# A two-block transformer layer in fp32 split products: weight splits placed first in each step, the second output projection ended tile by tile, the first expert's pieces in another order

## The chip, the cores and the metric

The kernel runs on one core of a Trainium2 chip. The metric is the device time of one execution in microseconds; the version before takes 806.64 us (median of three runs, 806.54 to 807.74). All times below are microseconds; those of the profile count from the start of the profiled execution's span.

## The reference

Two blocks in a row on 256 tokens of width 1024, in fp32. The first block (attention and retention, a convolutional feed-forward part) isn't touched by the change. The second ends like this:

```python
merged = gate_a * (o_a @ w_proj_a[l]) + gate_b * (o_b @ w_proj_b[l])
x = x + merged @ w_out[l]
x = x + hier_moe(rmsnorm_2(x, norm2_g[l]), w_router_group[l], b_router_group[l],
                 w_router_expert[l], b_router_expert[l], w_exp_gate[l], w_exp_up[l], w_exp_down[l])
return rmsnorm_2(x, final_norm_g)
```

`hier_moe` gives each token one of 4 groups by the router's group logits and weights of its two best experts within the group; each of the 16 experts is a gated unit (1024 to 256 twice, and 256 back to 1024).

## The kernel before

**Products.** A product in fp32 precision is three TensorE matmuls on rounded parts: `hi*hi`, `lo*hi`, `hi*lo` (`three`). For each weight quarter (128x1024 numbers) ScalarE writes the rounded `w_hi`, then another engine writes the rest, `w_lo = raw - w_hi`. Up to the end of the output projection GpSimd does the latter (L669); for the experts VectorE does (L3044), with ScalarE's part at L746. The matmuls of a quarter wait for its `lo`.

**Order.** Each engine has its own instruction list, written out by hand; engines meet by semaphores. An engine takes its list strictly in order, so an instruction whose semaphore is late holds all behind it.

**Output projection and router.** The second output projection (`token_quarter`, L1285) has 8 quarters of 12 matmuls for two tiles of 128 tokens (t = 0, 1) and two halves of the width (c = 0, 1; banks 2, 3 and 0, 1). After the seventh quarter TensorE transposes half c = 0 of `x` (`turn_half`, L1388), and after the eighth it runs the router products of k = 0 to 3 (L2025, L2027), transposes c = 1, and runs the router products of k = 4 to 7. VectorE adds the bank to `x` (L2425) and writes `h_lo` (L2242), ScalarE writes `h_hi` (L772). Matmuls whose results nobody reads (`keep_warm`, L1487) stand after the router and after the counting.

**Choice of groups.** From the logits VectorE finds each token's group (L2993 to L3019), TensorE counts the tokens of each group (`count_tokens`, L2042 to L2046), VectorE ranks the groups (L3023 to L3026) and sets `ranks_ready`. ScalarE and VectorE each load the rank's number into a register; ScalarE then splits the first expert's weights (L736, L738) and VectorE follows (L3037, and L3044 for its second quarter). After that VectorE works out each token's place in the sorted order (L3051 to L3060), the `one_hot` matrices (L3062) and the experts' weights (to L3100). Meanwhile ScalarE scales the rows of `x` (L1181), rounds them (L1184), and GpSimd writes their `lo` (L693). TensorE sorts the tokens with the one-hot matrices (`gather`, L2055).

**Experts.** There are 20 units (an expert with a tile of tokens; n = 0 to 19) and 120 steps p. A step is six matmuls of 128x512. Steps (n, 0) to (n, 3) are the up projections of unit n, (n, 4) and (n, 5) the down projections. After (n, 3) ScalarE takes the SiLU (L1208) and VectorE the product (L3122); TensorE transposes it (`turn_act`, L2100), ScalarE copies it (L1214) and VectorE writes its `lo` (L3128), for which (n, 4) waits. Between these pieces both engines split the quarters to come: quarter j at step `SPLIT_AT[j]`. A ring of 8 quarters holds them, so that j waits on ScalarE until quarter j - 8 is used up. Mostly one quarter is due per step. Units 6 and 7 (and 12 and 13) use the same weights one after the other; after these the ring frees late, and steps 53 and 89 have five splits each, 43 to 47 and 73 to 77. The transposes of units 8 and 14 stand at steps 54 and 90.

Of the kernel before, what the change touches and what calls it, by code (L numbers as in the profile page):

```python
# [141 lines left out]
GATHER_STEP = 4  # L142

# [211 lines left out]
def program(nc, weights, smalls, x_in, p_in, vec_in, rows, con_in, slot_in, pos_in, out):  # L355

    ctx = ExitStack()
    with ctx:
# [349 lines left out]
        def _(act_e):  # L708
# [458 lines left out]
            def left_squares(t):  # L1167

                act_e.wait_ge(sem("pair_free1"), 40)
                nc.scalar.activation(tok3[:, t, 0:512], x3[:, t, 0:512], ACT.Square, scale=D ** -0.5,  # L1170
                                     accum_out=stat[:, 8 + t:9 + t]).then_inc(sem("left_squares"), 1)

            for t in range(NT):
                left_squares(t)
            prepare_root()
            norm_hi(4, "norm2", range(4, KD))
# [95 lines left out]
        def _(pe):  # L1272
# [736 lines left out]
            for n, (c, f) in enumerate(WOUT2_ORDER):  # L2009
                if f == 0:  # L2010
                    await_pair(39 + c)
                pe.wait_ge(sem("merged_lo_done"), f + 1)
                token_quarter(4 * B_WOUT2 + n, 39 + c, f, (h_hi, h_lo))
                if n == 6:
                    await_read(39)
                    turn_half(4, 0)

            def router(ks):

                for k in ks:  # L2020
                    pe.wait_ge(sem("h_lo_done"), KD * 4 + k // 2 * 2 + 2)
                    at = slice(KD * 24 + 20 * k, KD * 24 + 20 * (k + 1))
                    for t in range(NT):
# [25 lines left out]
            keep_warm(1, 8, warm)  # L2049
# [123 lines left out]
        def _(dve):  # L2173
# [789 lines left out]
            def right_squares(t):  # L2963

                x = x3[:, t, 512:D]
                dve.wait_ge(sem("pair_free0"), 41 + t)
                link(V.tensor_tensor_reduce(tok3[:, t, 512:D], x, x, 1.0 / D, 0.0, ALU.mult, ALU.add, stat[:, t:t + 1]))
# [3 lines left out]
            add_pair(4 * B_WOUT2 + WOUT2_ORDER.index((1, 3)) + 1, 40, 1)  # L2971
            for t in range(NT):
                right_squares(t)
            dve.wait_ge(sem("left_squares"), NT)
            V.scalar_tensor_tensor(last_sums, stat[:, 8:10], RMS_EPS, stat[:, 0:2], ALU.add, ALU.add).then_inc(sem("last_summed"), 1)
            norm_lo(4, "norm2", range(4, KD))
# [12 lines left out]
            dve.wait_ge(sem("h_lo_done"), 5 * KD)  # L2989
# [56 lines left out]
            slot_low_first(chosen)  # L3046
            slot_low(1, chosen)

# [10 lines left out]
            link(V.tensor_tensor(near_place, place, near_rank, ALU.mult))  # L3059
            link(V.tensor_reduce(routed("slot"), near_place, AX_X, ALU.add))  # L3060
# [85 lines left out]
            for p in range(4, len(STEPS) - 1):  # L3146
                for n in range(len(UNITS)):
# [7 lines left out]
                if p == 5:  # L3155
                    slot_h_second(range(4, KD))
                for j in range(4, len(STREAM)):
                    if p == SPLIT_AT[j]:
                        slot_low(j)
                if p == step_of(0, 4):  # L3160
                    store_slot_weights()

# [60 lines left out]
```

## Time and profile before

| | |
|---|---|
| time, three runs | 806.64 (806.54 to 807.74) |
| the profiled execution's own time | 806.66 |
| its span | 804.7 |
| TensorE busy | 786.0 (98% of the span) |
| VectorE, ScalarE, GpSimd busy | 467.7, 435.8, 449.4 |
| mean granted TensorE clock | 0.993 of full speed |

The span is what the profiler saw between first and last instruction; the 1.96 us around it belong to the time too. TensorE's busy time includes matmuls that stream slowly, so the granted clock has to be read beside it.

### The profile page before, as it was taken

The numbers are of one execution on the slowest core, as the hardware profiler recorded it, in microseconds if no ns is written. First come the engines' busy times: TensorE is split into PE (matmuls) and PEld (weight loads), VectorE is DVE, ScalarE is ACT, GpSimd is POOL, SyncE is SP. The second block draws the span as 40 slices with busy tenths as digits, with TensorE's granted clock in tenths as the row PEclk, the third lists the DMA queues.
The fourth block names the chain that finished last, engine by engine and source line by source line (L and its number), as shares of the span: only waits on it lengthen the run. The fifth ranks groups of instructions, "written<-read, shape, count | busy, mean of one in ns | idle before, by whom it ended". The sixth has DMA issues, their size and how long they took to land.

```text
span 804.7 us, 15723 instructions
## 1 busy us (share of the span) xinstructions
PE 786.0 (98%) x6063; PEld 704.7 (88%) x6063; DVE 467.7 (58%) x947; ACT 435.8 (54%) x680; POOL 449.4 (56%) x351
## 2 busy tenths in 40 slices
PE   8999999999999999999999999999999899999996
PEld 7998889999999998889999999999978688788784
DVE  5853454672412215486498944437736896795874
ACT  5434654745545456785549534234427675673753
POOL 4997486999999998878974524245832000000002
PEclk9999999999999999999999999999998999999998
DMA  8765145455654555445663312233455796696811
GB/s 299 269 210 210 57 154 184 162 205 209 209 207 161 205 202 169 155 154 177 197 202 127 106 55 75 86 107 106 151 202 235 310 384 272 244 391 236 313 72 52
DMA packets 22810, 151.29 MB, mean 188 GB/s; under 512 B 2656, under 2 KB 3168, under 8 KB 5344
## 3 DMA queue, kind: packets, MB, share of 16 engines
q1 hardware_dynamic: 21312, 147.26, 50.2%
q10 hardware_dynamic: 1440, 3.21, 1.4%
q8 instruction: 42, 0.69, 0.3%
q14 instruction: 16, 0.13, 0.1%
HBM read 147.97 MB, written 1.05 MB: 185 GB/s over the span
## 4 chain that ended last, share of the span: by engine, by line
PE 93%; DVE 3%; ACT 1%; issue 1%; DMA 1%; ACTq 0%; DVEq 0%
PE bank L1285 77%; PE bank L1856 3%; DVE w_lo L3044 1%; PE bank L1388 1%; PE bank L1438 1%; PE bank L1452 1%; DMA vec<-vectors_dram 1%; PE bank L2100 1%; PE bank L1487 1%; PE bank L1885 0%; PE bank L1944 0%; PE bank L1866 0%; PE bank L2141 0%; PE bank L1461 0%; PE bank L1462 0%
## 5 line engine op out<-in xcount | busy, mean ns | idle before, releaser
L669 POOL TENSOR_TENSOR w_lo<-raw,w_hi 128x512 fp32r<-128x512 f32 x340 | 439.6, 1332 | 151.3 <-ACT w_hi L721 141.3
L1285 PE MATMUL bank<-h_hi,w_hi 128*128 128x256 f32 x800 | 227.3, 284 | 0.0
L1285 PE MATMUL bank<-h_hi,w_lo 128*128 128x256 f32 x800 | 222.3, 278 | 0.0
L1285 PE MATMUL bank<-h_lo,w_hi 128*128 128x256 f32 x788 | 218.4, 277 | 0.0
L721 ACT ACTIVATE w_hi<-raw 128x1024 fp32r<-128x1024 f32 x170 | 173.6, 1059 | 64.9 <-PE bank L1285 34.6
L1285 PEld LDWEIGHTS bank<-h_hi,w_hi 128*128 128x128 f32 x800 | 150.5, 188 | 4.2 <-issue 1.7
L1285 PEld LDWEIGHTS bank<-h_hi,w_lo 128*128 128x128 f32 x800 | 150.4, 188 | 0.0
L1285 PEld LDWEIGHTS bank<-h_lo,w_hi 128*128 128x128 f32 x788 | 148.1, 188 | 0.3
L1285 PE MATMUL bank<-w_hi,g 128*128 128x512 f32 x360 | 115.7, 391 | 3.4 <-issue 1.8
L700 POOL TENSOR_TENSOR tok<-x_sb,work 128x512 f32<-128x512 f32 x2 | 2.5, 1286 | 184.4 <-DVE x_sb L3166 184.4
L1285 PEld LDWEIGHTS bank<-w_hi,g 128*128 128x128 f32 x360 | 67.6, 188 | 18.2 <-issue 2.3
L1285 PE MATMUL bank<-w_hi,h_hi 128*128 128x512 f32 x184 | 73.4, 399 | 0.7 <-DVE w_lo L3037 0.6
L1285 PE MATMUL bank<-w_hi,h_lo 128*128 128x512 f32 x184 | 72.3, 393 | 0.0
L1285 PE MATMUL bank<-w_lo,h_hi 128*128 128x512 f32 x184 | 72.0, 392 | 0.0
L1285 PE MATMUL bank<-w_lo,g 128*128 128x512 f32 x180 | 70.2, 390 | 0.0
L2446 DVE TENSOR_TENSOR bank<-bank,work 128x512 f32<-128x512 f32 x11 | 7.7, 697 | 70.3 <-PE bank L1285 70.3
L3044 DVE TENSOR_TENSOR w_lo<-work,w_hi 128x1024 fp32r<-128x1024 f32 x39 | 45.7, 1220 | 3.0 <-ACT w_hi L746 2.6
L1285 PEld LDWEIGHTS bank<-w_hi,h_hi 128*128 128x128 f32 x184 | 34.6, 188 | 8.8 <-DVE w_lo L3037 1.0
L1285 PEld LDWEIGHTS bank<-w_hi,h_lo 128*128 128x128 f32 x184 | 34.6, 188 | 7.4
L1285 PEld LDWEIGHTS bank<-w_lo,h_hi 128*128 128x128 f32 x184 | 34.6, 188 | 6.9
L1285 PEld LDWEIGHTS bank<-w_lo,g 128*128 128x128 f32 x180 | 33.8, 188 | 6.6
L3044 DVE TENSOR_TENSOR w_lo<-raw,w_hi 128x1024 fp32r<-128x1024 f32 x32 | 37.7, 1219 | 2.8 <-ACT w_hi L746 2.6
(422 smaller groups left out, 1316.8 us busy)
## 6 DMA issues: line engine op xcount, KB each, us to landing
raw<-weights_dram SPq DMA_DIRECT2D x109, 1024.0 KB, 4.8
work<-weights_dram SPq DMA_DIRECT2D x27, 1024.0 KB, 6.8
x_sb<-x_dram SPq DMA_DIRECT2D x2, 512.0 KB, 4.5
raw<-weights_dram SPq DMA_DIRECT2D x2, 512.0 KB, 7.1
work<-final_norm_dram ACTq DMA_DIRECT2D x2, 512.0 KB, 4.3
work<-work ACTq DMA_DIRECT2D x8, 128.0 KB, 6.6
out_dram<-tok SPq DMA_DIRECT2D x3, 256.0 KB, 2.2
work<-constants_dram SPq DMA_DIRECT2D x1, 640.0 KB, 7.0
```

The lines of the kernel that those rows point to most:

```text
L669: return nc.gpsimd.tensor_tensor(w_lo[:, part], raw[:, part], w_hi[:, part].bitcast(F32), ALU.subtract)
L700: nc.gpsimd.tensor_tensor(tok3[:, 0, of], x3[:, 0, of], norm_row2[:, of], ALU.mult).then_inc(sem("first_gained"), 1)
L721: nc.scalar.activation(w_hi[:, ring(q)], raw[:, ring(q)], ACT.Copy).then_inc(sem("hi_done"), 1)
L1285: ins = mm(dst, a, b, start=start and n == 0, stop=stop and n == 2, skip_group_check=True)
L1388: ins = nc.tensor.transpose(bank[turned_bank(n, k)][:, k % 2 * S + t * P:k % 2 * S + (t + 1) * P], x3[:, t, k * P:(k + 1) * P], ident)
L1438: ins = mm(bank[4 + odd][:, t * P:t * P + (t + 1) * P], q3[own, f, t * P:(t + 1) * P], k3[own, kf(f), 0:(t + 1) * P], start=True, stop=True)
L1452: ins = nc.tensor.transpose(bank[6 + n % 2][:, i * P:(i + 1) * P], p[:, i * P:(i + 1) * P], ident)
L1487: mm(bank[to][:, 0:x.shape[1]], x[:, 0:P], x, start=True, stop=True, skip_group_check=True)
L1856: ins = mm(bank[b][rows, column + m * w:column + (m + 1) * w], lhs[rows, m, :], rhs[rows, m, :], start=True, stop=True)
L2100: ins = nc.tensor.transpose(to[:, k * P:(k + 1) * P], slot_act[:, k * P:(k + 1) * P], ident)
L2446: V.tensor_tensor(u_, u_, root_rows, ALU.mult).then_inc(sem("root_applied"), 1)
L3044: V.tensor_tensor(lo_, of, hi_.bitcast(F32), ALU.subtract).then_inc(sem("slot_lo_done"), 1)
```

## The change

Three things, and some small ones that go with them.

1. From step 10 on (`OPENED`), the splits of a step stand ahead of the other pieces of that step on ScalarE and VectorE. Before, they stood last.
2. The output projection's last two quarters of half c = 1 are done tile by tile: first tile 0 of both quarters, then tile 1, with the transposes of half c = 0 and of tile 0 between. `x`, `h_hi`, `h_lo` and the second half of the router follow tile by tile; ScalarE takes over tile 1's square of that half. The `keep_warm` behind the counting has 11 matmuls, not 8.
3. On VectorE, the arithmetic of the places stands ahead of the first expert's two quarters; in the first steps the product of unit 0 stands ahead of splits 4 and 5 and of the second half of `slot_lo`.

```diff
 # ScalarE, before the experts
+            act_e.wait_ge(sem("pair_free1"), 40)
+            for t in range(NT):
+                part_square(t, 0, stat[:, 8 + t:9 + t])
+            prepare_root()
             norm_hi(4, "norm2", range(4))
...
-            norm_hi(4, "norm2", range(4, KD))
+            act_e.wait_ge(sem("norm_turned"), 19)
+            for k in range(4, KD):
+                tile_hi(0, k, 6, k - 4)
+            act_e.wait_ge(sem("pair_free0"), 42)
+            part_square(1, 1, stat[:, 1:2])
+            for k in range(4, KD):
+                act_e.wait_ge(sem("norm_turned"), 20 + (k - 4) // 2)
+                tile_hi(1, k, (7, 0)[(k - 4) // 2], k % 2)
 # ScalarE, experts (VectorE has the same with slot_low)
             for p in range(4, len(STEPS) - 1):
+                splits = [j for j in range(4, len(STREAM)) if p == SPLIT_AT[j]]
+                if p >= OPENED:
+                    for j in splits:
+                        slot_hi_quarter(j)
                 for n in range(len(UNITS)):
...
-                for j in range(4, len(STREAM)):
-                    if p == SPLIT_AT[j]:
+                if p < OPENED:
+                    for j in splits:
                         slot_hi_quarter(j)
 # TensorE
+            for f in (2, 3):
+                ins = token_half(4 * B_WOUT2 + 4 + f, 40, f, 0)
+            ins.then_inc(sem("tile_ready"), 1)
+            await_read(39)
+            turn_half(4, 0)
+            token_half(4 * B_WOUT2 + 6, 40, 2, 1)
+            turn_tile(0, (6,))
+            token_half(4 * B_WOUT2 + 7, 40, 3, 1)
...
-            router(range(4))
-            await_read(40)
-            turn_half(4, 1)
-            router(range(4, KD)).then_inc(sem("logits_ready"), 1)
+            router(range(4), range(NT), lambda k: k // 2 * 2 + 2)
+            turn_tile(1, (7, 0))
+            router(range(4, KD), (0,), lambda k: 8)
+            router(range(4, KD), (1,), lambda k: 8 + (k - 4) // 2 * 2 + 2).then_inc(sem("logits_ready"), 1)
             keep_warm(1, 6, warm)
...
-            keep_warm(1, 8, warm)
+            keep_warm(1, 11, warm)
...
                     if n == 1:
                         pe.wait_ge(sem("slot_weights_ready"), 1)
-                        pe.wait_ge(sem("slot_h_lo"), KD)
 # VectorE, places and first expert
-            slot_low_first(chosen)
-            slot_low(1, chosen)
-
             dve.wait_ge(sem("counted"), 2)
             counts = bank[2][:, 0:NT * GROUPS].rearrange("p (t n) -> p t n", t=NT)
             V.tensor_tensor(near_place, counts, group_one, ALU.mult)
...
             link(V.tensor_tensor(near_place, place, near_rank, ALU.mult))
+            slot_low_first(chosen)
+            slot_low(1, chosen)
             link(V.tensor_reduce(routed("slot"), near_place, AX_X, ALU.add))
...
-                if p == 5:
-                    slot_h_second(range(4, KD))
-                for j in range(4, len(STREAM)):
-                    if p == SPLIT_AT[j]:
-                        slot_low(j)
                 if p == step_of(0, 4):
                     store_slot_weights()
+                if p == step_of(0, 5):
+                    slot_h_second(range(4, KD))
+                if p < OPENED:
+                    for j in [4] * (p == step_of(0, 3) + 1) + [5] * (p == step_of(0, 4)) + splits:
+                        if j not in (4, 5) or p > 6:
+                            slot_low(j)
```

The first place of which the prediction speaks is VectorE's list behind the ranking of the groups. `TENSOR_LOAD` is the load into the register, the `ISA` rows belong to it and to the address that it gives. Before:

```order
L3026 TENSOR_SCALAR work<-work 128x4
L3029 TENSOR_LOAD work
L3029 ISA x2
L3037 ISA
L3037 TENSOR_TENSOR w_lo<-work,w_hi 128x512
L3037 ISA
L3037 TENSOR_TENSOR w_lo<-work,w_hi 128x512
L3044 ISA
L3044 TENSOR_TENSOR w_lo<-work,w_hi 128x1024
L3051 TENSOR_TENSOR bank<-bank,work 128x8
L3052 TENSOR_TENSOR bank<-work 128x2x4
L3053 TENSOR_REDUCE work<-bank 128x2
```

The same place on VectorE after the change, with line numbers of the changed kernel:

```order
L3075 TENSOR_LOAD work
L3075 ISA x2
L3094 TENSOR_TENSOR bank<-bank,work 128x8
L3095 TENSOR_TENSOR bank<-work 128x2x4
L3096 TENSOR_REDUCE work<-bank 128x2
L3097 TENSOR_REDUCE work<-bank 128x2
L3099 TENSOR_TENSOR bank<-work 128x2x4
L3100 TENSOR_TENSOR bank<-work 128x8
L3101 TENSOR_TENSOR work<-bank,work 128x8
L3102 TENSOR_TENSOR bank<-work,bank 128x8
L3083 ISA
L3083 TENSOR_TENSOR w_lo<-work,w_hi 128x512
```

Eight small operations moved from behind the two quarters to ahead of them. Three of them (`bank<-work`) have both inputs in SBUF; so has `w_lo<-work,w_hi`.

The second place is VectorE at steps 52 to 56, around the transpose of unit 8. `g<-bank,g` is the `lo` of the transposed unit, `work<-bank,work` the product of a unit, `w_lo` and `w_more_lo` are splits. Before, from quarter 42 on:

```order
L3044 TENSOR_TENSOR w_lo<-raw,w_hi 128x1024 x2
L3044 TENSOR_TENSOR w_lo<-work,w_hi 128x1024 x2
L3044 TENSOR_TENSOR w_more_lo<-work,w_more_hi 128x1024 x2
L3128 TENSOR_TENSOR g<-bank,g 128x2x128
L3044 TENSOR_TENSOR w_lo<-work,w_hi 128x1024 x2
L3122 SCALAR_TENSOR_TENSOR work<-bank,work 128x256
```

After, at the same steps of VectorE:

```order
L3090 TENSOR_TENSOR w_lo<-raw,w_hi 128x1024 x2
L3090 TENSOR_TENSOR w_lo<-work,w_hi 128x1024 x2
L3090 TENSOR_TENSOR w_more_lo<-work,w_more_hi 128x1024 x2
L3090 TENSOR_TENSOR w_lo<-work,w_hi 128x1024
L3173 TENSOR_TENSOR g<-bank,g 128x2x128
L3090 TENSOR_TENSOR w_lo<-work,w_hi 128x1024
L3090 TENSOR_TENSOR w_lo<-raw,w_hi 128x1024
L3167 SCALAR_TENSOR_TENSOR work<-bank,work 128x256
```

Split 48 now stands ahead of the `lo` of unit 8, on ScalarE ahead of its copy too; steps 88 to 91 change in the same way.

The third place is VectorE from the end of `slot_lo`'s first half to the product of unit 1. Before:

```order
L3107 SCALAR_TENSOR_TENSOR slot_lo<-bank,vec,slot_hi 128x2x128 x4
L3044 TENSOR_TENSOR w_lo<-raw,w_hi 128x1024
L3107 SCALAR_TENSOR_TENSOR slot_lo<-bank,vec,slot_hi 128x2x128 x4
L3044 TENSOR_TENSOR w_lo<-raw,w_hi 128x1024
L3122 SCALAR_TENSOR_TENSOR work<-bank,work 128x256
L3128 TENSOR_TENSOR g<-bank,g 128x2x128
```

After, in the same stretch:

```order
L3152 SCALAR_TENSOR_TENSOR slot_lo<-bank,vec,slot_hi 128x2x128 x4
L3167 SCALAR_TENSOR_TENSOR work<-bank,work 128x256
L3090 TENSOR_TENSOR w_lo<-raw,w_hi 128x1024
L3173 TENSOR_TENSOR g<-bank,g 128x2x128
L3167 SCALAR_TENSOR_TENSOR work<-bank,work 128x256
L3188 COPY work<-bank 128x32
L3090 TENSOR_TENSOR w_lo<-raw,w_hi 128x1024
L3090 TENSOR_TENSOR w_more_lo<-raw,w_more_hi 128x1024
L3173 TENSOR_TENSOR g<-bank,g 128x2x128
L3152 SCALAR_TENSOR_TENSOR slot_lo<-bank,vec,slot_hi 128x2x128 x4
```

Two splits and four pieces of `slot_lo` moved from ahead of unit 0's product to behind it.

## Rows read from the trace of the kernel before

**Rows 1.** Page, busy time of each engine.
```profile
PE 786.0 (98%) x6063; PEld 704.7 (88%) x6063; DVE 467.7 (58%) x947; ACT 435.8 (54%) x680; POOL 449.4 (56%) x351
```
**Rows 2.** Stretches; columns: stretch, us, busy us of each engine, PEclk, DMA.
```profile
602.00:604.00 2.00, 1.79 (x9) 1.79 (x9) 1.57 (x8) 0.39 (x2) 0.00 (x0) 0.51 0.03 8
...
608.00:609.00 1.00, 1.00 (x7) 0.90 (x5) 0.00 (x0) 0.01 (x1) 1.00 (x2) 0.58 0.00 0
...
640.00:660.00 20.00, 20.00 (x93) 16.40 (x92) 20.00 (x23) 15.70 (x21) 0.00 (x0) 1.00 1.00 395
```
**Rows 3.** Timeline, TensorE, 598 to 631 us.
```profile
599.71 1.09 PE L1388 MATMUL bank<-con,x_sb 128*128 128x128 f32 x8
602.21 0.40 PE L2025 MATMUL bank<-sm,h_hi 128*128 128x40 f32 x1 [1.40 <-DVE h_lo L2242]
605.65 2.91 PE L1487 MATMUL bank<-g 128*128 128x512 f32 x6
608.35 0.75 PE L2042 MATMUL bank<-work 128*128 128x4 f32 x4
612.33 0.51 PE L1285 MATMUL bank<-w_hi,h_hi 128*128 128x512 f32 x1 [0.60 <-DVE w_lo L3037]
630.07 0.44 PE L2100 MATMUL bank<-con,work 128*128 128x128 f32 x2 [2.63 <-DVE work L3122]
```
**Rows 4.** Timeline, VectorE, ranking and first splits.
```profile
602.86 0.16 DVE L2197 RECIPROCAL stat<-stat 128x2 f32<-128x2 f32 x1
609.62 0.17 DVE L3026 TENSOR_SCALAR work<-work 128x4 int32<-128x4 int32 x1
611.58 1.29 DVE L3037 TENSOR_TENSOR w_lo<-work,w_hi 128x512 fp32r<-128x512 f32 x2 [1.79 <-ACT w_hi L736]
614.17 0.17 DVE L3051 TENSOR_TENSOR bank<-bank,work 128x8 f32<-128x8 f32 x1
615.41 0.17 DVE L3060 TENSOR_REDUCE work<-bank 128x2 f32<-128x8 f32 x1
```
**Rows 5.** Timeline, ScalarE: first split of the experts, SiLU of unit 0.
```profile
610.78 1.15 ACT L736 ACTIVATE w_hi<-work 128x512 fp32r x2 [2.77 <-DVE work L3026]
626.10 0.47 ACT L1208 ACTIVATE work<-bank,stat 128x256 f32<-128x256 f32 x1 [0.58 <-PE bank L1285]
```
**Rows 6.** Timeline, GpSimd and VectorE: small operations with and without GpSimd beside them.
```profile
605.96 4.99 POOL L693 TENSOR_TENSOR slot_lo<-tok,g 128x512 fp32r<-128x512 f32 x4 [14.62 <-ACT g L1184]
...
363.57 10.50 POOL L669 TENSOR_TENSOR w_lo<-raw,w_hi 128x512 fp32r<-128x512 f32 x8
364.81 0.17 DVE L2581 TENSOR_TENSOR soft_a<-small_tok,vec 128x16 f32<-128x16 f32 x1
365.00 1.15 DVE L2582 SCALAR_TENSOR_TENSOR soft_b<-soft_a 128x16 f32<-128x16 f32 x1
369.96 1.22 DVE L2587 TENSOR_TENSOR decay_g<-decay_g,rate 128x16 f32<-128x16 f32 x1
```
**Rows 7.** Timeline, VectorE, 624 to 645 us.
```profile
629.54 0.48 DVE L3122 SCALAR_TENSOR_TENSOR work<-bank,work 128x256 f32<-128x256 f32 x1
635.87 6.89 DVE L3044 TENSOR_TENSOR w_lo<-work,w_hi 128x1024 fp32r<-128x1024 f32 x6
644.95 0.48 DVE L3122 SCALAR_TENSOR_TENSOR work<-bank,work 128x256 f32<-128x256 f32 x1
```
**Rows 8.** Timeline, transpose of unit 2 on TensorE.
```profile
645.76 0.38 PE L2100 MATMUL bank<-con,work 128*128 128x128 f32 x2
```
**Rows 9.** Timeline, around unit 8's transpose, and TensorE's wait for unit 14.
```profile
700.61 0.35 ACT L1214 CAST g<-bank 128x256 fp32r<-128x256 f32 x1
702.63 0.42 DVE L3128 TENSOR_TENSOR g<-bank,g 128x256 fp32r<-128x256 f32 x1
703.15 0.47 PE L1285 MATMUL bank<-w_hi,g 128*128 128x512 f32 x1 [1.64 <-issue]
755.57 0.50 PE L1285 MATMUL bank<-w_hi,g 128*128 128x512 f32 x1 [1.60 <-DVE g L3128]
```

More of the change, by code:

```diff
@@ L142 @@
 GATHER_STEP = 4
+OPENED = 10
 WOUT_ORDER = ((0, 0), (0, 1), (1, 0), (1, 1), (0, 2), (0, 3), (1, 2), (1, 3))
@@ L1164, in _, with part_square, tile_hi @@
                 hi(q + LEAD)
-            norm_hi(4, "norm2", range(4))
[L1167 to L1175, printed above, removed]
-            norm_hi(4, "norm2", range(4, KD))
+            def part_square(t, c, to):
+                x = slice(c * 512, (c + 1) * 512)
+                nc.scalar.activation(tok3[:, t, x], x3[:, t, x], ACT.Square, scale=D ** -0.5, accum_out=to)\
+                    .then_inc(sem("left_squares"), 1)
+            def tile_hi(t, k, b, j):
+                nc.scalar.activation(h_hi[:, k, t * P:(t + 1) * P], bank[b][:, j * P:(j + 1) * P], ACT.Copy, scale=v("norm2", k))\
+                    .then_inc(sem("h_hi_done"), 1)
+            act_e.wait_ge(sem("pair_free1"), 40)
+            for t in range(NT):
+                part_square(t, 0, stat[:, 8 + t:9 + t])
+            prepare_root()
+            norm_hi(4, "norm2", range(4))
+            act_e.wait_ge(sem("norm_turned"), 19)
[6 more added lines that the diff above has]
+                tile_hi(1, k, (7, 0)[(k - 4) // 2], k % 2)
             act_e.wait_ge(sem("last_summed"), 1)
@@ L2012, in _, with turn_tile, router @@
                 pe.wait_ge(sem("merged_lo_done"), f + 1)
[L2013 to L2018, printed above, removed]
+                if n < 6:
+                    token_quarter(4 * B_WOUT2 + n, 39 + c, f, (h_hi, h_lo))
+            def turn_tile(t, to):
+                pe.wait_ge(sem("pair_free0"), 41 + t)
+                for i, b in enumerate(to):
+                    n = 4 // len(to)
+                    for j in range(n):
+                        k = 4 + i * n + j
+                        ins = nc.tensor.transpose(bank[b][:, j * P:(j + 1) * P], x3[:, t, k * P:(k + 1) * P], ident)
+                    ins.then_inc(sem("norm_turned"), 1)
+            for f in (2, 3):
[6 more added lines that the diff above has]
+            token_half(4 * B_WOUT2 + 7, 40, 3, 1)
+            def router(ks, tiles, ready):
                 for k in ks:
-                    pe.wait_ge(sem("h_lo_done"), KD * 4 + k // 2 * 2 + 2)
+                    pe.wait_ge(sem("h_lo_done"), KD * 4 + ready(k))
                     at = slice(KD * 24 + 20 * k, KD * 24 + 20 * (k + 1))
-                    for t in range(NT):
+                    for t in tiles:
                         own, dst = slice(t * P, (t + 1) * P), bank[2][:, 64 * t:64 * t + 40]
@@ L2962, in _, with add_tile, tile_lo @@
             merged_low(3)
[L2963 to L2967, printed above, removed]
-            add_pair(4 * B_WOUT2 + WOUT2_ORDER.index((0, 3)) + 1, 39, 0)
-            norm_lo(4, "norm2", range(4))
[L2971 to L2974, printed above, removed]
+            def add_tile(t):
+                V.tensor_tensor(x3[:, t, 512:D], pair(40)[t][:, :], x3[:, t, 512:D], ALU.add).then_inc(sem("pair_free0"), 1)
+            def tile_lo(t, k, b, j):
+                own = slice(t * P, (t + 1) * P)
+                V.scalar_tensor_tensor(h_lo[:, k, own], bank[b][:, j * P:(j + 1) * P], v("norm2", k),
+                                       h_hi[:, k, own].bitcast(F32), ALU.mult, ALU.subtract).then_inc(sem("h_lo_done"), 1)
+            add_pair(4 * B_WOUT2 + WOUT2_ORDER.index((0, 3)) + 1, 39, 0)
+            dve.wait_ge(sem("tile_ready"), 2)
+            add_tile(0)
+            dve.wait_ge(sem("pair_free0"), 41)
+            x = x3[:, 0, 512:D]
+            link(V.tensor_tensor_reduce(tok3[:, 0, 512:D], x, x, 1.0 / D, 0.0, ALU.mult, ALU.add, stat[:, 0:1]))
+            norm_lo(4, "norm2", range(4))
+            dve.wait_ge(sem("quarter_done"), N_QUARTERS)
+            add_tile(1)
+            dve.wait_ge(sem("h_hi_done"), KD * 4 + 8)
+            for k in range(4, KD):
+                tile_lo(0, k, 6, k - 4)
+            dve.wait_ge(sem("left_squares"), NT + 1)
             V.scalar_tensor_tensor(last_sums, stat[:, 8:10], RMS_EPS, stat[:, 0:2], ALU.add, ALU.add).then_inc(sem("last_summed"), 1)
-            norm_lo(4, "norm2", range(4, KD))
+            for k in range(4, KD):
+                dve.wait_ge(sem("h_hi_done"), KD * 4 + 8 + (k - 4) // 2 * 2 + 2)
+                tile_lo(1, k, (7, 0)[(k - 4) // 2], k % 2)
             dve.wait_ge(sem("last_rooted"), 1)
@@ L2988, in _ @@
             parts = bank[2][:, 0:64 * NT].rearrange("p (t n) -> p t n", t=NT)
-            dve.wait_ge(sem("h_lo_done"), 5 * KD)
+            dve.wait_ge(sem("h_lo_done"), 5 * KD + 4)
             V.memset(routed("keys"), 0.0)
@@ L3146, in _ @@
             for p in range(4, len(STEPS) - 1):
+                splits = [j for j in range(4, len(STREAM)) if p == SPLIT_AT[j]]
+                if p >= OPENED:
+                    for j in splits:
+                        slot_low(j)
                 for n in range(len(UNITS)):
```

1 line of the change is left out of this document (added).

## The prediction

> **What bounds the kernel now.** I read the busy times first: TensorE is busy for 786.0 of 804.7 [rows 1], so at most 19 can be won by filling its gaps, plus what it loses at the lower clock. The stretches then show where: only behind the output projection is the granted clock down, 0.51 of full at 602 to 604 and back within 608 to 609 [rows 2]. That is the level of 1.2 GHz after 2.4 GHz; ahead of the fall TensorE had done the router's narrow products and transposes and had waited 1.40 [rows 3]. Third, TensorE's timeline: waits of 1.40, 0.60 and 2.63 between 601 and 630 [rows 3], and two of 1.64 and 1.60 at 703 and 756 [rows 9]. Fourth, the timelines of VectorE and ScalarE say what ends these waits. From 611.58 on VectorE has hardly a hole; it is busy 20.00 of 20 in 640 to 660 [rows 2]. So from there to unit 2 it is VectorE that sets the pace, and TensorE's transposes of unit 2 start at 645.76, just 0.33 behind the end of their product (644.95 + 0.48) [rows 7, 8].
>
> **Part 2, the projection by tiles.** The number of matmuls stays. TensorE's last products of the projection end some 0.5 later, as four transposes (half of the 1.09 in [rows 3]) now stand between them: near 598.5, if I take 599.71 less 16 router products of 0.11 (half of the 3.44/16 = 0.215 that they take at the low clock, 602.21 to 605.65 [rows 3]) and add the 0.5. Then 16 products to 600.2, tile 1's four transposes to 600.75, tile 0's eight products to 601.65. Beside it VectorE adds tile 1 (0.65, as a 128x512 operation in [rows 4]) and writes tile 0's pieces. A 128x128 piece isn't in the trace; it lies between 0.17 (small, [rows 4]) and 0.48 (128x256, [rows 7]), and I take 0.28. ScalarE's four for tile 1, from 600.8, and VectorE's behind them then end at 602.5. The root's reciprocal follows at 602.5 instead of 602.86 [rows 4], and the last four products run to 603.4 instead of 605.65, if the clock falls at 602 as before: 2.2 earlier. The six filler matmuls take 2.70 at 1.2 GHz (605.65 to 608.35 [rows 3]), to 606.1; the group flag is there by then. So counting starts 2.2 earlier, and the ranks are known at 607.5 instead of 609.79 [rows 4]. With piece costs at the two ends this is 0.4 more or less.
>
> **Part 3, the places ahead of the first splits.** VectorE waits 1.79 before L3037, until ScalarE has loaded the rank and rounded the first half (610.78 is 0.99 behind the ranks) [rows 4, 5]. The eight operations take 1.24 (614.17 to 615.41 [rows 4]), and TensorE needs nothing of them until the gather, 5.6 later. VectorE loads the same register first, though; its load isn't shown, lies between 0 and ScalarE's 0.99, and I take 0.9. Places start at 608.4 and by themselves would end at 609.65, some 0.55 behind ScalarE's first half (608.5 + 0.58, [rows 5]). The first expert would start 1.9 earlier than 612.33.
>
> But GpSimd is at work there. Its four operations (L693) run 605.96 to 610.95 [rows 6], directly behind ScalarE's rounded rows, thus with the root 0.36 earlier: 605.6 to 610.6, ends at 606.85, 608.1, 609.35, 610.6. Before, VectorE's first operation with two inputs in SBUF came at 611.58, behind all of this. Elsewhere small VectorE operations take 1.15 and 1.22 beside running GpSimd, where another of the same size takes 0.17 [rows 6]: they waited for GpSimd's operation to end. Not each one waits (the one at 364.81 didn't). The moved operations hold three with both inputs in SBUF, and the split behind them is one too. Played through from 608.4: the second of the eight waits to 609.35; the fifth, due at 609.75, waits behind GpSimd's last to 610.7; the other three end at 611.4. The first split starts at 611.4, not 609.65, and the first expert at 612.2: 0.15 earlier. If VectorE comes before 608.1, it waits at 608.1, at 609.45 and with the split itself until 610.8: 0.8 earlier. I take 0.15 to 0.8.
>
> The Trainium skill ("SBUF — State Buffer", section on SBUF's two separate sides) says that a VectorE operation with two SBUF inputs and a GpSimd operation exclude each other for the whole instruction. The trace agrees with 1.15 and 1.22 against 0.17. Without the rule the sum below would come out 1.5 lower.
>
> **Part 3, the first unit.** Call u the shift of the first expert's start, now -0.15. The products of steps 0 to 7 and the gather keep their length. The SiLU of unit 0 runs at 625.95 to 626.4 instead of 626.10 [rows 5]. The places being done, VectorE's chain up to the first half of `slot_lo` ends 1.6 earlier, at 624.1, and waits there for the SiLU. The product of unit 0 starts at 626.45 instead of 629.54 [rows 7]: the wait of 2.63 is gone. What is late next is VectorE. Behind 626.45 stand, at its spacings (a split 1.14, six in 6.89 [rows 7]; product 0.40; `lo` of a unit 0.34; a `slot_lo` piece 0.40): product 0 and split 4 to 628.0, `lo` 0 and product 1 with the copy to 628.9, splits 5 and 6 to 631.2, `lo` 1 to 631.5, four `slot_lo` pieces to 633.1, and splits 7 to 15 to 643.35. TensorE could have begun unit 2's transposes near 642.7: the four down steps run from 628.5 to 634.4, six up steps of six matmuls at 0.23 follow. The product would end at 643.8 without part 1. With it split 16 stands first: 645.0. So they start at 645.05, not 645.76: 0.7 earlier at u = -0.15, and 1.35 earlier at u = -0.8. TensorE's freed 2.63 comes back as a wait of some 2.4 here. The removed wait for `slot_h_lo` costs nothing, as those four pieces are done at 633.1, when TensorE comes to unit 2.
>
> **Part 1, splits first.** Where ScalarE and VectorE have time, the order changes nothing for TensorE, which had no wait between 645 and 700. At step 54 they have none: ScalarE comes from splits 43 to 47 straight to the copy of unit 8 at 700.61, VectorE to its `lo` at 702.63, and TensorE starts at 703.15 [rows 9], 0.10 behind that `lo`'s end. Now split 48 stands ahead on both. ScalarE's is done in time; VectorE's adds 1.14. Step 90 is the same with split 78, and TensorE's wait of 1.60. Thus 2 x 1.14 = +2.3. The burst itself starts when the ring frees, which goes with TensorE, so an earlier start doesn't shorten it. DMA isn't late here: ScalarE ran the next splits without a hole.
>
> **The sum.** -0.7 and +2.3 give +1.6; with u = -0.8, -1.35 and +2.3 give +0.95. In the middle +1.25 on the profiled execution's own 806.66 (span 804.7), which lies at the median of 806.64: 807.9.
>
> **Rivals.**
> - *GpSimd doesn't hold VectorE.* For it: one of the small operations didn't wait [rows 6], and VectorE may come late in GpSimd's work. Against: 1.15 and 1.22. Then u = -1.9, unit 2 is 2.45 earlier, and the sum is -0.15: 806.5. If the clock also stays at 2.4 GHz (the router's products 0.4 shorter, the fillers half), VectorE is there another 1.0 earlier: 805.5.
> - *The bursts cost nothing more.* For it: the first of these waits is put down to "issue" [rows 9]. Against: the other names L3128, and both starts lie right behind it. Without +2.3 the time is 805.6 with GpSimd's hold and 804.2 without: faster. It needs both to be wrong.
> - *Slower: the clock falls under the first expert.* The fillers behind the counting end near 609.9 (11 of 0.23 from 607.4), and the first product comes at 612.2: 2.3 of nothing, behind a thin stretch. For it: a wait of 1.40 behind narrow products went ahead of the fall at 602. Against: 2.63 with dense products ahead of it at 627 did no harm. In the low stretch TensorE does half: of the 6.8 us from 602.0 to 608.8 that is 3.4, and if it is back after half as long, 1.7. The first unit is TensorE's own, so this passes through in full: 807.9 + 1.7 = 809.6, up to 811.3. It decides once u is above -0.8 and the clock in 612 to 616 is below 1.
>
> The Trainium skill ("TensorE: Matmul & The Clock Gate", the part on HAM oscillation) says that waits between bursts of matmuls can throttle the clock anew, which is this last rival; the row of 602 agrees that waits and thin work go ahead of a fall.
>
> **How the numbers follow.** A measurement here can't tell less than 0.2% (1.6) from no change. Chances: the forecast 0.50 (807.6 to 808.3, with scatter a third of it above 808.25); GpSimd doesn't hold 0.22, of which 0.05 below 805.0; bursts without cost 0.13, of which 0.08 below 805.0; the clock 0.15, nearly all slower. Slower: 0.17 + 0.13 = 0.30. Faster: 0.13, and 0.02 for what I haven't seen: 0.15. Same: 0.55. The range of 8 in 10 runs from 804.9 (the faster cases in part) to 809.8 (the clock at its lower price).
>
> **What would show it.** Right: VectorE's small `bank<-work` operations near 608 to 611 take about 1 us instead of 0.17; the first expert starts between 611.5 and 612.2; the wait at 627 is gone, and one of about 2.4 stands before unit 2's transposes at 644.4 to 645.1; the waits at steps 56 and 92 are 2.8, not 1.6. Wrong: the first expert before 611, no wait at unit 2, a low clock anywhere behind 612, or waits of 1.6 at those two steps.

## The result, and the profile after

The changed kernel took 813.15 us (median of 5 runs, 812.32 to 813.72) where the kernel before took 806.92 (5 runs beside them, 806.54 to 808.91). The ratio is 1.0072, with a 95% interval of 1.0057 to 1.0088: slower by 0.7%. The forecast was 807.9 with a range up to 809.8, so the time lies outside.

The profiled execution took 813.72, its span is 811.7. TensorE's busy time, the row that answers to [rows 1], has grown by 6.0, with three matmuls more in the records:
```profile
PE 792.0 (98%) x6066; PEld 709.9 (87%) x6066; DVE 466.8 (58%) x949; ACT 440.9 (54%) x686; POOL 450.0 (55%) x351
```
All but the three added fillers is the same work; a TensorE that is longer busy with it ran at a lower clock in places. The stretches (columns as in [rows 2]) show where:
```profile
8.00:12.00 4.00, 4.00 (x20) 3.77 (x19) 2.53 (x6) 3.49 (x8) 0.80 (x1) 0.57 1.03 432
...
604.00:606.00 2.00, 2.00 (x12) 1.79 (x13) 1.77 (x12) 1.00 (x1) 0.00 (x0) 0.88 0.00 0
...
610.00:612.00 2.00, 2.00 (x6) 1.57 (x5) 1.74 (x7) 1.98 (x4) 2.00 (x2) 0.50 0.71 172
...
646.00:648.00 2.00, 2.00 (x9) 1.64 (x8) 2.00 (x3) 1.33 (x2) 0.00 (x0) 0.62 0.97 356
648.00:650.00 2.00, 2.00 (x7) 1.53 (x6) 1.80 (x4) 1.06 (x1) 0.00 (x0) 0.53 1.02 422
...
760.00:762.00 2.00, 2.00 (x5) 1.57 (x6) 2.00 (x3) 0.54 (x1) 0.00 (x0) 0.50 0.99 365
762.00:764.00 2.00, 2.00 (x6) 1.56 (x5) 1.68 (x3) 1.06 (x1) 0.00 (x0) 0.50 1.01 369
764.00:766.00 2.00, 2.00 (x6) 1.52 (x6) 1.03 (x1) 0.72 (x1) 0.00 (x0) 0.51 1.02 397
```
Before, the clock was down behind the projection only [rows 2]. Now it is down behind the first constants, behind the projection, at 646 to 650 (unit 2) and at 759 to 766 (step 92). PEclk 0.50 is 1.2 of 2.4 GHz, and the counts behind TensorE's busy time say what that does: at 0.50 it begins 5 or 6 of its 128x512 matmuls in 2 us, where at the full clock they begin 0.23 apart.

TensorE's timeline (start, us, line, operation, and in brackets the wait ahead) names what stood ahead of each fall:
```profile
7.71 3.26 PE L1405 MATMUL bank<-con,x_sb 128*128 128x128 f32 x16 [1.94 <-DMA vec<-vectors_dram]
...
596.24 1.04 PE L1405 MATMUL bank<-con,x_sb 128*128 128x128 f32 x8
...
609.04 4.30 PE L1504 MATMUL bank<-g 128*128 128x512 f32 x11
613.19 0.40 PE L1302 MATMUL bank<-w_hi,h_hi 128*128 128x512 f32 x1
...
629.43 0.47 PE L1302 MATMUL bank<-w_hi,g 128*128 128x512 f32 x1 [0.20 <-DVE g L3173]
...
645.79 0.44 PE L2131 MATMUL bank<-con,one_hot 128*128 128x128 f32 x2 [2.12 <-DVE work L3167]
646.07 0.38 PE L2134 MATMUL bank<-con,work 128*128 128x128 f32 x2
...
706.22 0.47 PE L1302 MATMUL bank<-w_hi,g 128*128 128x512 f32 x1 [2.77 <-issue]
...
759.75 0.80 PE L1302 MATMUL bank<-w_hi,g 128*128 128x512 f32 x1 [2.73 <-DVE g L3173]
```
The same places in the kernel before, the first two not shown until now:
```profile
6.70 1.97 PE L1388 MATMUL bank<-con,x_sb 128*128 128x128 f32 x16 [0.97 <-DMA vec<-vectors_dram]
...
594.37 1.03 PE L1388 MATMUL bank<-con,x_sb 128*128 128x128 f32 x8
```
Set side by side, place by place, these rows are the balance of the two executions:

- At 594.37 and 596.24 stand the transposes of half c = 0; of the change only the order of the 12 matmuls just ahead of them differs. This execution is already 1.87 late: a DMA at the start landed 1.0 later, and the clock fell behind that wait. Nothing of the change stands at the start, and in the other thirteen profiles of this document these transposes start between 593.9 and 594.6, those with the changed order among them, so I take it for chance. Which of the unprofiled executions had such a start, their times alone don't say (the kernel before spreads from 805.4 to 809.6 in all its runs).
- Unit 2's transposes: 646.07 against 645.76 [rows 8]. (The row of 645.79 is the `one_hot` transposes, which stand ahead of them in both kernels.) Parts 2 and 3 have won 1.56 on the way, though Part 1 stands in this stretch too.
- Step 56: 706.22 against 703.15 [rows 9], 2.76 more lost. 1.13 is the longer wait (2.77 for 1.64), the other 1.6 the low clock of 646.5 to 649.9.
- Step 92: 759.75 against 755.57 [rows 9], 1.11 more: the second longer wait (2.73 for 1.60).
- The end: 811.7 against 804.7, 2.8 more, in the low stretch of 759 to 766.

The sum: 1.87 - 1.56 + 2.76 + 1.11 + 2.8 = 7.0, the difference of the spans. Without the start it is 5.1, of which 4.4 is clock (1.6 and 2.8). The ratio of 1.0072, which is 5.8 us, lies between the two sums.

VectorE's timeline at the places, the stretch of [rows 4] now, with GpSimd's four operations:
```profile
607.32 4.99 POOL L694 TENSOR_TENSOR slot_lo<-tok,g 128x512 fp32r<-128x512 f32 x4 [14.11 <-ACT g L1197]
...
608.42 0.19 DVE L3072 TENSOR_SCALAR work<-work 128x4 int32<-128x4 int32 x1
609.58 0.17 DVE L3094 TENSOR_TENSOR bank<-bank,work 128x8 f32<-128x8 f32 x1 [0.96 <-PE bank L2080]
...
610.15 0.94 DVE L3099 TENSOR_TENSOR bank<-work 128x8 f32<-128x8 f32 x1
611.01 0.16 DVE L3100 TENSOR_TENSOR bank<-work 128x8 f32<-128x8 f32 x1
...
611.74 1.73 DVE L3083 TENSOR_TENSOR w_lo<-work,w_hi 128x512 fp32r<-128x512 f32 x2 [0.16 <-DVE bank L3102]
```
With GpSimd at work from 607.32 for 4.99, one of two alike small operations (L3099, L3100) takes 0.94, and the pair of first splits 1.73 instead of 1.29.

### The profile page after: what moved, and what is told of

The parts are those of the page before. It is cut to its first block, busy times and chain, and to the rows that moved or that the text cites. A ratio compares the mean times of both kernels' runs of the same rounds, so it can differ in the third digit from the quotient of the medians.

```text
span 811.7 us, 15735 instructions
## 1 busy us (share of the span) xinstructions
PE 792.0 (98%) x6066; PEld 709.9 (87%) x6066; DVE 466.8 (58%) x949; ACT 440.9 (54%) x686; POOL 450.0 (55%) x351
## 4 chain that ended last, share of the span: by engine, by line
PE 93%; DVE 4%; ACT 1%; DMA 1%; issue 1%; ACTq 0%
PE bank L1302 77%; PE bank L1873 3%; DVE w_lo L3090 2%; PE bank L1504 1%; PE bank L1405 1%; PE bank L1455 1%; DMA vec<-vectors_dram 1%; PE bank L1469 1%; DVE w_more_lo L3090 1%; PE bank L1902 0%; PE bank L2089 0%; PE bank L2134 0%; PE bank L1961 0%; PE bank L1883 0%; PE bank L2174 0%
## 5 line engine op out<-in xcount | busy, mean ns | idle before, releaser
L1302 PE MATMUL bank<-w_hi,g 128*128 128x512 f32 x360 | 117.7, 397 | 5.7 <-DVE g L3173 2.9
L747 ACT ACTIVATE w_hi<-work 128x1024 fp32r<-128x1024 f32 x38 | 39.5, 1056 | 8.5 <-PE bank L1302 8.2
```

Of the source, the lines that this page charges most:

```text
L747: nc.scalar.activation(hi_, of, ACT.Copy).then_inc(sem("slot_hi_done"), 1)
L1302: ins = mm(dst, a, b, start=start and n == 0, stop=stop and n == 2, skip_group_check=True)
```

## Experiments

My theory was then: Part 1 lengthens TensorE's waits, and behind the lengthened ones the clock falls. The rivals: the falls come from Parts 2 and 3, or from the shifted start. Each ratio below is to runs of the kernel before on the same chip, whose medians were 807.25 (for no_first, first_only, tiles_only and filled), 807.79 (turns_first, product_first, few_warm and no_hold) and 807.76 (filled_bursts, late_hold, turns_all and best). The profile shows one execution of each; the mean granted clock is on record for all (over the whole span, the stretches in which TensorE has nothing to do included).

**Part 1 undone (no_first).**
```
-OPENED = 10
+OPENED = 200
```


> The changed kernel with OPENED = 200: the splits stand behind the other pieces again from step 10 on (Part 1 undone), Parts 2 and 3 stay. Theory (the longer waits of Part 1 let TensorE's clock fall at unit 2 and at step 92): the waits at steps 56 and 92 go back to about 1.6, no low stretch stands between 620 and 795, the wait before unit 2's transposes is about 1.0 instead of 2.12. From 813.15: -2.3 (two waits), -1.1 (unit 2), -1.7 and -3.4 (clock): about 804.6, and less than before's 806.9. Rival (the falls come from Part 2 and 3, through the earlier arrival at unit 2 or a different phase): the falls stay, only the 3.4 of waits go: about 809.7.

Measured: 805.32, ratio 0.9970 (0.9959 to 0.9981). The waits are back at 1.6 and 1.6, the one at unit 2 is 1.00, and behind 612 the clock stays whole until TensorE's work ends. The changed kernel lies 1.0072 - 0.9970 = 0.0102 above, 8.2 us: 2.3 and 1.1 of waits and 4.8 that the waits don't explain. The rival's 809.7 is out. Part 1 alone made the kernel slower; Parts 2 and 3 make it 0.3% faster. The mean granted clock says the same of every execution: 0.984 to 0.990 in the five of the changed kernel (mean 0.9876), 0.991 to 0.995 in the eleven of no_first (mean 0.9928). A clock lower by 0.0052 over a span of some 805 is 4.2 us, near the 4.8.

**Part 1 alone (first_only).** The kernel before, with the loop of ScalarE as below and that of VectorE in the same way.
```
+OPENED = 10
...
             for p in range(4, len(STEPS) - 1):
+                splits = [j for j in range(4, len(STREAM)) if p == SPLIT_AT[j]]
+                if p >= OPENED:
+                    for j in splits:
+                        slot_hi_quarter(j)
...
-                for j in range(4, len(STREAM)):
-                    if p == SPLIT_AT[j]:
+                if p < OPENED:
+                    for j in splits:
                         slot_hi_quarter(j)
```

> The kernel before with Part 1 alone (splits first from step 10). Theory (waits lengthened by Part 1 let the clock fall): waits of 2.8 at steps 56 and 92, a new one of 1.1 before unit 2's transposes, and a low stretch of up to 6.8 us behind one of the two long ones at a cost of 3.4: 806.9 + 2.3 + 1.1 + 3.4 = 813.7. If the waits are too short by themselves for a fall (rival: Part 2 or 3 is needed): 810.3 with no low stretch between 620 and 795.

Measured: 813.48, ratio 1.0073 (1.0049 to 1.0096). The sum is right, its parts are not all. TensorE's waits are 2.78 at step 56 and 2.73 at step 92, but none stands before unit 2: there the clock was down instead, behind the wait of 1.76 at 629.65. The stretches of its profile:
```profile
626.00:630.00 4.00, 2.23 (x13) 1.55 (x11) 3.59 (x7) 0.48 (x1) 0.00 (x0) 1.00 0.87 346
630.00:632.00 2.00, 2.00 (x11) 1.90 (x11) 1.01 (x3) 1.69 (x3) 0.00 (x0) 0.54 0.78 217
632.00:636.00 4.00, 4.00 (x12) 3.12 (x11) 1.60 (x3) 1.36 (x3) 0.00 (x0) 0.50 0.37 158
...
758.00:760.00 2.00, 0.00 (x0) 0.00 (x0) 2.00 (x3) 2.00 (x3) 0.00 (x0) 0.96 1.00 422
760.00:762.00 2.00, 1.71 (x4) 1.42 (x5) 2.00 (x3) 1.08 (x2) 0.00 (x0) 0.50 1.02 418
```
A TensorE at half speed came to unit 2 no earlier than VectorE, and so didn't wait. Parts 2 and 3 aren't needed for the slowdown. But of the two falls here only the one at step 92 stands behind a wait that Part 1 lengthened: the wait at 629.65 stands at the place of the 2.63 of the kernel before.

**Part 2 alone (tiles_only).** The changed kernel with Parts 1 and 3 taken out:
```
-OPENED = 10
+OPENED = 200
...
                         pe.wait_ge(sem("slot_weights_ready"), 1)
+                        pe.wait_ge(sem("slot_h_lo"), KD)
...
+            slot_low_first(chosen)
+            slot_low(1, chosen)
+
             dve.wait_ge(sem("counted"), 2)
...
-            slot_low_first(chosen)
-            slot_low(1, chosen)
...
+                if p == 5:
+                    slot_h_second(range(4, KD))
+                for j in splits:
+                    slot_low(j)
                 if p == step_of(0, 4):
                     store_slot_weights()
-                if p == step_of(0, 5):
-                    slot_h_second(range(4, KD))
-                if p < OPENED:
-                    for j in [4] * (p == step_of(0, 3) + 1) + [5] * (p == step_of(0, 4)) + splits:
-                        if j not in (4, 5) or p > 6:
-                            slot_low(j)
```

> The kernel before with Part 2 alone (projection ended tile by tile, 11 filler matmuls behind the counting instead of 8). Theory: the ranks come about 1.9 earlier, but the first expert still waits for ScalarE's and VectorE's first splits behind GpSimd; unit 2 stands behind VectorE's full row from 611 on, which starts at most 1.9 earlier: 805.0 to 806.9, and no low stretch behind 620. Rival (the thinner work behind the projection is what unsettles the clock later): a low stretch between 620 and 795 and over 808.

Measured: 806.10, ratio 0.9969 (0.9957 to 0.9982). It is as fast as Parts 2 and 3 together (no_first), so that Part 3 by itself adds nothing that can be measured. Its profile shows two other things. First, in this execution the clock fell at 628, behind a wait of 2.46. The kernel before has the same wait there, of 2.63, and in its profile no fall came behind it [rows 3]:
```profile
628.63 0.68 PE L2134 MATMUL bank<-con,work 128*128 128x128 f32 x2 [2.46 <-DVE work L3169]
...
647.11 0.38 PE L2134 MATMUL bank<-con,work 128*128 128x128 f32 x2
```
```profile
630.00:632.00 2.00, 2.00 (x7) 1.80 (x8) 1.54 (x3) 1.03 (x2) 0.00 (x0) 0.50 0.90 377
```
This fall wasn't free: unit 0's transposes start 1.44 earlier than in the kernel before (628.63 against 630.07), unit 2's 1.35 later (647.11 against 645.76), 2.8 between the two. The profiled execution is also the slowest of the nine (808.04). So a fall can come without Part 1; over all executions the mean clock here is that of the kernel before, 0.9916 against 0.9914.

Second, with the places back behind the splits, it is the two halves of the first split that GpSimd holds, 2.92 instead of 1.29:
```profile
608.76 2.92 DVE L3084 TENSOR_TENSOR w_lo<-work,w_hi 128x512 fp32r<-128x512 f32 x2 [1.79 <-ACT w_hi L737]
```

**The waits filled (filled).** Is it the idleness, or only the time that passes? TensorE adds zeros to a bank while it waits:
```
+        nothing = sb("nothing", P, F32R)[:, :]
...
+            def add_nothing(count):
+                for i in range(count):
+                    mm(bank[7][:, 0:S], nothing, h_hi[:, 0, :], start=False, stop=False, skip_group_check=True)
...
+                        if m == 2:
+                            add_nothing(9)
                         turn_act(m)
...
+                for m, count in ((8, 10), (14, 10)):
+                    if p == step_of(m, 4):
+                        add_nothing(count)
...
+            V.memset(nothing.bitcast(F32), 0.0)
```


> The changed kernel with small matmuls that add zero to a bank in use, put into TensorE's three waits: 9 before unit 2's transposes, 10 each before the down steps 56 and 92 (0.11 to 0.23 us each at the high clock). The waits themselves stay as long. Theory (a wait is what lets the clock fall): no low stretch between 620 and 795, and 1.7 + 3.4 less than 813.15: about 808.0. Rival (the falls follow something other than these waits): they stay and the time is 813 or a little more, by what the fillers overrun.

Measured: 808.66, ratio 1.0012 (1.0001 to 1.0023), 0.0060 or 4.8 us below the changed kernel. The fillers took 1.24 (nine) and 1.36 (ten). VectorE and ScalarE come as late as before: from the last product ahead of step 56 to the first behind the wait it is 3.17 in both kernels (701.02 to 704.19, and 703.05 to 706.22). But only 1.06, 1.58 and 1.53 of the waits stay idle:
```profile
643.06 1.24 PE L2107 MATMUL bank<-h_hi,nothing 128*128 128x256 f32 x9
645.36 0.44 PE L2137 MATMUL bank<-con,one_hot 128*128 128x128 f32 x2 [1.06 <-DVE work L3179]
```
```profile
646.00:648.00 2.00, 2.00 (x11) 1.62 (x10) 2.00 (x4) 1.89 (x3) 0.00 (x0) 1.00 1.00 324
...
758.00:760.00 2.00, 2.00 (x10) 1.59 (x10) 2.00 (x3) 1.08 (x2) 0.00 (x0) 1.00 0.99 336
```
The clock is whole where it had been at 0.62 and 0.50. Work that computes nothing, and is 29 matmuls more, makes the kernel 4.8 us faster. The mean clock of its twelve executions is 0.9931, 0.991 at the lowest, where the changed kernel's highest is 0.990; by the means that is 4.4 us. What is left over no_first, 1.0012 - 0.9970 or 3.4 us, is the lengths of the waits, 2.3 + 1.1.

**Two of the three filled (filled_bursts).** As above, without the nine before unit 2.

> The changed kernel with the matmuls that add zero in front of the down steps 56 and 92 only, none before unit 2. Theory (each wait opens the way for its own fall): the low stretch behind unit 2's wait can stay (1.7), the one at step 92 goes (3.4); between 808.7 (filled) and 813.15, near 810.4. Rival (only the sum of idle time matters, or one of the two falls brings the other): the time is that of filled, 808.7.

Measured: 810.08, ratio 1.0023 (1.0010 to 1.0037); in the profile the low stretch behind unit 2 is back (PEclk 0.52 in 646 to 648, behind a wait of 2.12) and the one at step 92 is not. Each wait has its own fall. The difference to filled is 0.9 us, less than the 1.7; the intervals of the two overlap, so the size of this one is open. The mean clock, 0.9904 against filled's 0.9931, would make it 2.2.

**Turns ahead of the last splits of a burst (turns_first).** If the splits ahead of the turn are what TensorE waits for, the opposite of Part 1 must help. On top of no_first:
```
 SPLIT_AT = [max(split_before(j), 0) for j in range(len(STREAM))]
+for j_ in (46, 47, 76, 77):
+    SPLIT_AT[j_] += 1
```


> Part 1 undone and at the two bursts the opposite of it: splits 46, 47, 76 and 77 move one step back, so that ScalarE's copy and VectorE's `lo` of units 8 and 14 stand ahead of the last two splits of the burst and not behind all five. Splits 46 and 47 are needed at steps 58 and 59 only. Theory (the waits at steps 56 and 92 are the copy and `lo` standing behind splits, 1.14 each): both waits of 1.6 go, 805.3 - 3.2 = 802.1. Rival (the burst as a whole is late, its order doesn't matter): the waits move to steps 57 to 59 and the time stays within 1 of 805.3.

Measured: 803.35, ratio 0.9945 (0.9926 to 0.9963). Between theory and rival: both waits of 1.6 are gone, and two of 0.68 stand one unit later, at steps 62 and 98:
```profile
708.68 0.50 PE L1304 MATMUL bank<-w_hi,g 128*128 128x512 f32 x1 [0.68 <-DVE g L3175]
```
VectorE is still full there, and the next unit's turn stands behind a split again; turns_all below moves that one too.

**The product of unit 2 ahead of two splits (product_first).** On turns_first:
```
+for j_ in (14, 15):
+    SPLIT_AT[j_] = 16
```

> As the one ahead, and splits 14 and 15 (needed at steps 20 and 21) behind the product of unit 2 at step 16 instead of ahead of it. Theory (the wait of 1.00 before unit 2's transposes is VectorE's row with those two splits in it): this wait goes, another 0.7 to 1.0 less: about 801.2. Rival (VectorE is full there, so what is moved is missed a step later): the wait comes back before the down steps of unit 2 and nothing is won: 802.1.

Measured: 802.84, ratio 0.9936 (0.9919 to 0.9953). The wait of 1.00 is gone, one of 0.49 stands before the down steps. The step from turns_first is inside both intervals; in the waits it is 0.5.

**Fewer fillers behind the counting (few_warm).** On no_first:
```
-            keep_warm(1, 11, warm)
+            keep_warm(1, 9, warm)
```

> Part 1 undone and 9 filler matmuls behind the counting instead of 11. The 11 run at the lower clock there, 0.39 each, and end at 611.28 where VectorE's first half of the split ends at 610.7. Theory (the fillers end last): the first expert starts 0.6 earlier, 805.3 - 0.6 = 804.7. Rival (the shorter cover lets the clock stay down longer, half of each us lost): 805.3 to 807.

Measured: 803.73, ratio 0.9956 (0.9939 to 0.9974), which overlaps with no_first. In the profiles the first expert starts at 610.94 instead of 611.28, and unit 2's transposes at 642.58 instead of 642.72: 0.1, not 0.6. Inconclusive as a gain.

**GpSimd moved away from the places (no_hold).** On no_first, 6 fillers and
```
                     pool.wait_ge(sem("tok_hi_done"), t + 1)
+                    pool.wait_ge(sem("slot_lo_done"), 2)
...
-            keep_warm(1, 11, warm)
+            keep_warm(1, 6, warm)
```


> Part 1 undone, 6 fillers instead of 11, and GpSimd's four operations (the tokens' second halves) start behind VectorE's second split instead of beside the places; they are needed at the gather only, 7 us later. Theory (a VectorE operation with two inputs in SBUF is held by a running GpSimd operation): L3099 takes 0.17 instead of 0.93, the pair of first splits 1.29 instead of 1.72, the first half of the split is ready near 609.5 instead of 610.7; with the fillers ending at 609.5 the first expert starts 1.2 to 1.7 earlier: 803.6 to 804.1. Rival (these two are long for another reason): they stay as they are and the time is about 804.7. If GpSimd then holds VectorE's work of 612 to 617, this shows as long operations there, covered by VectorE's wait at 626.

Measured: 804.06, ratio 0.9953 (0.9935 to 0.9970), within the interval of no_first. VectorE's rows:
```profile
608.21 0.17 DVE L3100 TENSOR_TENSOR bank<-work 128x8 f32<-128x8 f32 x1
...
609.03 1.30 DVE L3084 TENSOR_TENSOR w_lo<-work,w_hi 128x512 fp32r<-128x512 f32 x2 [0.16 <-DVE bank L3103]
...
611.57 2.79 DVE L3108 TENSOR_SCALAR one_hot<-work 128x256 fp32r<-128x256 f32 x2
614.28 1.26 DVE L3110 TENSOR_SCALAR work<-work 128x8 f32<-128x8 f32 x1
```
0.94 became 0.17 and 1.73 became 1.30: the hold is GpSimd's. But it was moved, not removed: `one_hot` took 2.79 instead of 0.62 and L3110 1.26. The first expert started at 609.85, 1.43 earlier than in no_first, and unit 2's transposes only 0.15 earlier (642.57): 0.6 went to the low clock, which lasted until 611 and so covered the first three products. The other 0.7 went behind the gather, to two of VectorE's splits that came late behind the held operations (the larger part at 623.09, where a product starts 0.61 behind the one ahead of it instead of 0.23). The late `one_hot` itself was there in time.

**GpSimd behind `one_hot` (late_hold).** On no_hold:
```
-                    pool.wait_ge(sem("slot_lo_done"), 2)
+                    pool.wait_ge(sem("one_hot_ready"), NT)
```

> Part 1 undone, 6 fillers, and GpSimd's four operations behind the `one_hot` pair instead of behind the second split: in no_hold they held that pair (2.79 instead of 0.61) and L3110 (1.26), and TensorE then waited for `one_hot` and a split what it had won. Theory: the pair takes 0.61 again, the gather's second pass at 617.85 just finds the halves ready, and the down steps start 0.4 to 0.6 earlier than the 627.34 of no_hold; another 0.5 less than no_hold. Rival (the gather now waits for GpSimd, or the next split is held by it): no difference from no_hold.

Measured: 804.17, ratio 0.9950 (0.9931 to 0.9969): the rival, no difference. The pair takes 0.62 again, but the gather's second pass waits 0.20 for GpSimd, and in the profiled execution the clock was down until 612. The hold has moved on once more, to the next split and a small operation with two inputs in SBUF (0.17 elsewhere):
```profile
613.23 6.04 POOL L695 TENSOR_TENSOR slot_lo<-tok,g 128x512 fp32r<-128x512 f32 x4 [22.09 <-DVE one_hot L3108]
...
616.17 1.94 DVE L3091 TENSOR_TENSOR w_lo<-raw,w_hi 128x1024 fp32r<-128x1024 f32 x1
618.03 1.26 DVE L3124 TENSOR_TENSOR work<-work 128x16 f32<-128x16 f32 x1
```

**All turns ahead of what isn't needed yet (turns_all).** no_first with
```
+for j_ in (46, 47, 53, 76, 77, 83):
+    SPLIT_AT[j_] += 1
+for j_ in (14, 15):
+    SPLIT_AT[j_] = 16
+for j_ in (16, 17):
+    SPLIT_AT[j_] = 18
```


> As product_first, and splits 53 and 83 (needed at steps 65 and 101) behind the turns at steps 60 and 96, splits 16 and 17 behind the turn at 18. Theory: VectorE is full behind the bursts and behind unit 2, so what is needed first must stand first; the waits of 0.71, 0.72 and 0.49 that were left go: 802.8 - 1.9 = 900.9 less 100, that is 800.9. Rival (each one comes back a unit later): 802.8.

(The sum there is 802.8 - 1.9 = 800.9; the figures between are a slip.) Measured: 800.76, ratio 0.9908 (0.9890 to 0.9927). The theory holds: TensorE has no wait of 0.3 or more between 602 and its last units, and it is busy without a hole in the three stretches where it had waited:
```profile
640.00:655.00 15.00, 15.00 (x72) 12.11 (x70) 14.82 (x18) 12.79 (x16) 0.00 (x0) 1.00 1.02 385
700.00:712.00 12.00, 12.00 (x55) 9.93 (x54) 12.00 (x13) 10.88 (x14) 0.00 (x0) 1.00 0.99 371
756.00:768.00 12.00, 12.00 (x55) 9.71 (x54) 12.00 (x14) 10.40 (x13) 0.00 (x0) 1.00 0.72 281
```
VectorE is as full there as ever (12.00 of 12). Not one operation was taken from it; only the order is another.

**Both together (best).** turns_all with late_hold's edits.

> turns_all and late_hold together: the gains stand at different places and add up, 800.9 - 0.5 = 800.4. Rival (the earlier start is given back at the low clock or before unit 2): that of turns_all.

Measured: 799.90, ratio 0.9899 (0.9880 to 0.9918): 1.0% faster than the kernel before, 1.7% faster than the changed one. Over turns_all it is 0.9, with overlapping intervals: what late_hold's part adds isn't shown. In its profile the gather's second pass waits 0.58 for GpSimd.

## Why the prediction was wrong, point by point

The times of the changed kernel in this section are less 1.87, the start's chance.

- *Part 2.* Right in the mechanism: the reciprocal at 602.34 (forecast 602.5), the ranks at 606.74 (forecast 607.5 with 0.4 more or less, which was 0.8 too late). The clock fell later than I took it to, behind the router's last products instead of ahead of them.
- *Part 3, GpSimd's hold.* The hold is there, and no_hold and tiles_only show its cause. One small operation was held (0.94), and the split behind. But the first expert started at 611.32, 1.0 earlier, not 0.15 to 0.8, and what ended last was not the split: the 11 fillers at 0.39 each ended there. I had set them down as ending at 609.9, at the full clock.
- *Part 3, the first unit.* Right in the mechanism: the wait at 627 is 0.20, VectorE is late next, and unit 2's wait is 2.12 (forecast 2.4). Unit 2 starts 1.56 earlier, not 0.7 to 1.35. Those two figures are themselves 0.3 too high: 645.05 follows the product's end by less than 0.1, where [rows 7, 8] have 0.33 between the two. The `one_hot` transposes stand between, and the forecast set their start against that of the next ones. Put right, its sum would have been near +1.5 instead of +1.25.
- *Part 1, the two bursts.* Right in length: 2.77 and 2.73, together 2.26 more (forecast 2.28). That each is a split of 1.14 standing ahead of the turn is shown by turns_first and turns_all.
- *The step that failed is the sum.* It took every longer wait at its own length, "2 x 1.14 = +2.3", and "TensorE's freed 2.63 comes back as a wait of some 2.4 here". At three places Part 1 put 1.1 more of idleness in front of dense matmuls (2.12, 2.77 and 2.73 for the 1.00, 1.6 and 1.6 of no_first); in the profile two of the three cost 1.6 and 2.8 more in the clock behind them. filled shows it: 4.8 us come back when the idleness is cut, with the waits' ends where they were.
- *The rival that had the mechanism had the wrong place.* I gave the clock 0.15, under the first expert alone, and dismissed it elsewhere by one row: "2.63 with dense products ahead of it at 627 did no harm". That row was one draw: it shows one execution. tiles_only's execution has the same wait, at 2.46, with the clock at 0.50 behind it, and first_only's at 1.76.

Without the falls my sum would have been near: -1.56 and +2.26 make +0.7 where I forecast +1.25.

What stays open is when a wait lets the clock fall. In the profiles here, behind dense matmuls, it fell behind 1.76, 2.12 (twice), 2.46 and 2.73 (twice), and not behind 2.63, 2.77 and 2.78, nor behind any of 1.64 or less. So the length isn't all; the rest was not tried. Open too is the size of the fall at unit 2 (1.6 in the balance, 0.9 by the times of filled and filled_bursts, 2.2 by their mean clocks).

## What to carry to other kernels

A longer wait of a TensorE that is otherwise dense isn't priced by its length: here 3.4 us of longer waits brought 4.8 us of low clock, and one harmless wait in a single trace is no evidence against it. The mean clock of every execution, where it is on record, is better evidence than one profile. Where two engines work through a row that is full, order it by when TensorE needs each piece: turns ahead of splits that are due two or more steps later gave 0.6%, the splits ahead of the turn cost 1.0%. And a moved operation that blocks another engine blocks whatever stands beside it next; look for its new neighbours first.

## What the runs showed of the hardware

- The clock went to 1.2 GHz inside work that is dense but for one wait of 1.76 to 2.73, for 3.4 (646.5 to 649.9) to 6.9 us (759.1 to 766.0). A handful of matmuls that add zero, 1.2 to 1.4 us in a wait of that kind, kept it up in the profile of filled, and the mean clock of all twelve executions agrees (0.9931 against 0.9876).
- GpSimd's 128x512 subtractions (4.99 for four) held not only VectorE's operations with two inputs in SBUF, but a TENSOR_SCALAR from SBUF to SBUF too: 2.79 for a pair that takes 0.62, and 1.26 for one of 0.17 in no_hold. VectorE's small operations with an input or the output in PSUM beside it mostly took their 0.15 to 0.20, but L3099 (SBUF to PSUM) took 0.94 in the changed kernel, where L3100, like it, took 0.16. GpSimd's own four took longer too where VectorE's work stood beside them: 6.04 in late_hold.
